# Inverting the unit triangles of a chunked delta rule column by column, with one product for the transposes of inverse and carried matrix

## The reference

```python
def step(state, inp):
    r_t, w_t, k_t, v_t, a_t, b_t = inp
    sa = jnp.einsum('bhvk,bhk->bhv', state, a_t)
    state = (state * w_t[:, :, None, :]
             + sa[..., None] * b_t[:, :, None, :]
             + v_t[..., None] * k_t[:, :, None, :])
    y_t = jnp.einsum('bhvk,bhk->bhv', state, r_t)
    return state, y_t
```

## Time and profile before

| | us |
|---|---|
| median of 3 runs | 2226.78 |
| lowest, highest | 2226.38, 2231.42 |
| profiled execution | 2220.09 |
| its span, first to last instruction | 2218.3 |

### The profile page before, as it was taken

How to read it: one execution, slowest core, us unless ns; L and a number is a source line. 1 busy time by engine, 2 the same in 40 slices (tenths; PEclk the granted TensorE clock), 3 DMA queues, 4 the chain that set the end, 5 groups by cost and what they waited for, 6 DMA issues and landing times.

```text
span 2218.3 us, 37433 instructions
## 1 busy us (share of the span) xinstructions
PE 2005.0 (90%) x15948; PEld 1570.5 (71%) x15948; DVE 792.4 (36%) x1248; ACT 812.1 (37%) x1061; POOL 777.7 (35%) x644
## 2 busy tenths in 40 slices
PE   5997976668999999989999899999999999979987
PEld 3666866643778888866667478888887886768767
DVE  5586443324332221014766632222102223324333
ACT  6766133332244343122247534343312423242232
POOL 3353322210334443433432034444444433234432
PEclk8998999986899999999999899999999999989988
DMA  5111000010223333222121022333223121131211
GB/s 154 57 50 63 2 5 5 4 48 23 59 75 94 99 90 109 95 80 67 65 69 39 0 76 76 97 92 102 97 91 106 60 77 57 39 100 58 77 38 58
DMA packets 190138, 147.16 MB, mean 66 GB/s; under 512 B 6826, under 2 KB 188289, under 8 KB 190004
## 3 DMA queue, kind: packets, MB, share of 16 engines
q1 hardware_dynamic: 190004, 145.18, 21.2%
HBM read 143.07 MB, written 2.10 MB: 65 GB/s over the span
## 4 chain that ended last, share of the span: by engine, by line
PE 79%; DVE 7%; ACT 5%; issue 5%; POOL 2%; DMA 1%; SPq 0%; DVEq 0%; ACTq 0%
PE psum L2479 21%; PE psum L2481 20%; PE psum L2480 20%; PE psum L2634 4%; POOL w_lo L1099 2%; ACT w_hi L1220 1%; DVE X_lo L1773 1%; PE psum L2555 1%; PE psum L2485 1%; PE psum L2859 1%; PE psum L2920 1%; PE psum L2933 1%; PE psum L2850 1%; PE psum L3030 1%; DVE col L2230 0%
## 5 line engine op out<-in xcount | busy, mean ns | idle before, releaser
L1099 POOL TENSOR_TENSOR w_lo<-weight_raw,w_hi 128x256 fp32r<-128x256 f32 (+5 forms) x588 | 706.1, 1233 | 1236.5 <-ACT w_hi L1220 1236.4
L2479 PE MATMUL psum<-X_hi,w_hi 128*128 128x512 f32 x1400 | 577.4, 412 | 26.3 <-DVE X_lo L1773 17.8
L2481 PE MATMUL psum<-X_hi,w_lo 128*128 128x512 f32 x1400 | 552.3, 395 | 0.0
L2480 PE MATMUL psum<-X_lo,w_hi 128*128 128x512 f32 x1400 | 551.9, 394 | 0.0
L1220 ACT ACTIVATE w_hi<-weight_raw 128x2048 fp32r<-128x2048 f32 (+2 forms) x134 | 249.5, 1862 | 362.9 <-PE psum L2481 338.3
L2479 PEld LDWEIGHTS psum<-X_hi,w_hi 128*128 128x128 f32 x1400 | 266.5, 190 | 126.8 <-issue 53.8
L2480 PEld LDWEIGHTS psum<-X_lo,w_hi 128*128 128x128 f32 x1400 | 266.8, 191 | 58.7 <-issue 7.5
L2481 PEld LDWEIGHTS psum<-X_hi,w_lo 128*128 128x128 f32 x1400 | 266.3, 190 | 58.1
L2479 PE MATMUL psum<-w_hi,X_hi 128*128 128x256 f32 x640 | 191.4, 299 | 13.0 <-DVE X_lo L1773 10.8
L2480 PE MATMUL psum<-w_lo,X_hi 128*128 128x256 f32 x640 | 185.1, 289 | 0.0
L2481 PE MATMUL psum<-w_hi,X_lo 128*128 128x256 f32 x640 | 184.9, 289 | 0.0
(11 more groups left out here) (465 smaller groups left out, 2566.3 us busy)
## 6 DMA issues: line engine op xcount, KB each, us to landing
weight_raw<-in_ffn_w_gu SPq DMA_DIRECT2D x88, 512.0 KB, 4.8
weight_raw<-in_l_w_in SPq DMA_DIRECT2D x45, 512.0 KB, 4.7
weight_raw<-in_ffn_w_down SPq DMA_DIRECT2D x40, 512.0 KB, 3.6
weight_raw<-in_kv_w SPq DMA_DIRECT2D x16, 512.0 KB, 4.5
weight_raw<-in_l_w_out SPq DMA_DIRECT2D x16, 512.0 KB, 4.5
weight_raw<-in_rw_w_k SPq DMA_DIRECT2D x8, 512.0 KB, 6.6
weight_raw<-in_rw_w_r SPq DMA_DIRECT2D x8, 512.0 KB, 4.0
weight_raw<-in_rw_w_v SPq DMA_DIRECT2D x8, 512.0 KB, 4.0
```

The lines of the kernel that those rows point to most:

```text
L1099: ins = pool.tensor_tensor(l, r, h.bitcast(F32), ALU.subtract)
L2479: pe.matmul(ps, wh, xh, start=start, stop=False, skip_group_check=True)
L2480: pe.matmul(ps, wh, xl, start=False, stop=False, skip_group_check=True)
L2481: return pe.matmul(ps, wl, xh, start=False, stop=stop, skip_group_check=True)
```

## The change

The triangle is inverted in another way. At level lv (0 to 5) blocks of 2^lv are joined to blocks of 2^(lv+1). A matrix N is carried along; the factor of a level is N under a mask that keeps the identity and takes away the pairs to be joined, `(j == i) - pair(n)`. Multiplying by this factor moves both the inverse and N one level on. So N of level lv (TensorE) times the factor gives the next factor under the next mask (VectorE), and one product, T, multiplies the factor with the transposes of inverse and N side by side: 128 columns instead of 64.

- AtX and its masks go. At is masked into the first stacked tile `TN0`, whose other part is the identity, written once by ScalarE; An is masked into the first factor, and VectorE adds the identity over 128x1024.
- N at levels 0 to 4, T at levels 0 to 5; T is 128 columns wide at levels 0 to 3, 64 at levels 4 and 5. Before, there were G and T at levels 1 to 5.
- The At copy on ScalarE and GpSimd's four level masks a tile go, with the semaphores for them. GpSimd's four identity additions stay, now before N0.
- The list of slots is rewritten; AV moves to the weight_raw region.

```diff
-LEVELS = (4, 8, 16, 32)
-CORE_MASKS = ("incl", "strict", "four_t", "four_n", "eye", "lv2", "lv3", "lv4", "lv5")
+LEVELS = (2, 4, 8, 16, 32)
+CORE_MASKS = ("incl", "strict", "minus", "pair0", "pair1", "pair2", "pair3", "pair4", "pair5")
...
-        "start": [("AtX", tt), ("An", tt), ("At", tt)],
+        "start": [("At", tt), ("An", tt)],
...
-    for name in ("start", "X0", "G1", "U0", "T1", "SY0", "G2", "YS0", "T2", "bt", "G3", "X1", "T3", "U1", "G4", "SY1",
-                 "T4", "YS1", "Ak", "G5", "Rb", "T5", "AV", "Rk", "kt"):
+    for name in ("start", "X0", "N0", "U0", "T0", "SY0", "N1", "YS0", "T1", "bt", "N2", "X1", "T2", "U1", "N3", "SY1",
+                 "T3", "YS1", "N4", "Ak", "T4", "Rb", "T5", "AV", "Rk", "kt"):
...
             for tt in range(TT):
-                wait_job(pool, ("AtX", tt))
+                wait_job(pool, ("At", tt))
                 for g in range(2):
                     for slot in range(2):
-                        part = TT2[1][:, g, slot, 1, :, :]
-                        pool.tensor_tensor(part, part, mask("eye", 4), ALU.add).then_inc(f_ready, 1)
-                pool.wait_ge(at_copied, tt + 1)
-                for lv in range(2, NLV + 1):
-                    if lv >= 3:
-                        wait_done(pool, ("G", tt, lv - 2, 1))
-                    elif tt:
-                        wait_done(pool, ("G", tt - 1, 4, 1))
-                    pool.tensor_tensor(whole(Lm[(lv + 1) % 2]), whole(At), mask(f"lv{lv}"),
-                                       ALU.mult).then_inc(level_ready, 1)
+                        part = TN0[:, g, slot, 1, :, :]
+                        pool.tensor_tensor(part, part, TN0[:, g, slot, 0, :, :], ALU.add).then_inc(unit_ready, 1)
...
+                        if what == "An":
+                            link(ins)
+                            dve.wait_ge(eye_ready, 1)
+                            every = Gs[0][:, :, :, :, :].rearrange("p g b k c -> p (g b) (k c)")
+                            ins = dve.tensor_tensor(every, every, TN0[:, :, :, 0, :, :].rearrange(
+                                "p g b k c -> p (g b) (k c)"), ALU.add)
...
+                        if what == "N":
+                            ins = product64(
+                                lambda q, r, k: psum[to(q, r)[0], b + to(q, r)[1], CH * k:CH * k + CH],
+                                lambda q, r, k: both[rows(q, r), g, level_slot(lv, q, r), 1, k, :],
+                                lambda q, r, k: factor[rows(q, r), g, level_slot(lv, q, r), k, :], ks=range(4))
+                        elif lv < NLV - 2:
+                            ins = product64(
+                                lambda q, r, k: psum[to(q, r)[0], b + to(q, r)[1], :].rearrange(
+                                    "p (t k c) -> p t k c", t=2, k=4)[:, :, k, :],
+                                lambda q, r, k: factor[rows(q, r), g, level_slot(lv, q, r), k, :],
+                                lambda q, r, k: both[rows(q, r), g, level_slot(lv, q, r), :, k, :], ks=range(4))
```

More of the change, by code:

```diff
@@ L100, in host_constants, with pair @@
     j, i = p[:, None] % 64, np.arange(64)[None, :]
[L101 to L104, removed]
+    def pair(n):
+        return 1.0 * ((j // (2 * n) == i // (2 * n)) & (j % (2 * n) >= n) & (i % (2 * n) < n))
+    masks = [j <= i, j < i, -1.0 * (j < i), pair(1)] + [(j == i) - pair(n) for n in LEVELS]
     lv = np.stack(masks, 1).astype(np.float32)
@@ L361, in core_slots @@
     mine = {
-        "start": [("AtX", tt), ("An", tt), ("At", tt)],
+        "start": [("At", tt), ("An", tt)],
         "Ak": [("Ak", tt)], "AV": [("AV", tt)], "Rb": [("Rb", tt)], "Rk": [("Rk", tt)], "kt": [("kt", tt)],
     }
-    for lv in range(1, NLV + 1):
-        for kind in "GT":
+    for lv in range(NLV):
+        for kind in "NT" if lv < NLV - 1 else "T":
             mine[f"{kind}{lv}"] = [(kind, tt, lv, 0), (kind, tt, lv, 1)]
@@ L403, in make_jobs @@
                 j.add(("bonus",), 5, "A")
-            elif what == "AtX":
-                j.add(("AtX", n), low, "D")
+            elif what == "At":
+                j.add(("At", n), low, "D")
             elif what == "An":
                 j.add(("An", n), high, "D")
[L408 to L411, removed]
+            elif what == "N":
+                j.add(("N", n, *lv), high if lv[1] else low, "D")
             elif what == "T":
@@ L910, in mask, with unit_mask, stacked @@
             return lvl[:, at_:at_ + 1, :].to_broadcast([P, n, CH])
-        def inverse(lv, g, kind):
-            return TT2[lv % 2][:, g, :, kind, :, :]
+        def unit_mask(name):
+            return lvl[:, None, CORE_MASKS.index(name), None, :].to_broadcast([P, 2, 4, CH])
+        def stacked(lv):
+            return TN0 if lv == 0 else TN[(lv + 1) % 2]
         def split_k(ap, g):
@@ L1472, in _ @@
             rn = xf[0:16, 1, :]
-            act.wait_ge(lvl_in, 16)
+            act.wait_ge(lo_ready, PL.first_slot["v"] + PL.count["v"])
+            for h in range(2):
+                at_ = CST["ident"] + CH * h
+                ins = act.activation(TN0[halves(h), :, :, 0, :, :].rearrange("p g b k c -> p (g b) k c"),
+                                     cst[halves(h), None, None, at_:at_ + CH].to_broadcast([CH, 4, 4, CH]), ACT.Copy)
+            ins.then_inc(eye_ready, 1)
             for tt in range(TT + 1):
@@ L2058, in _ @@
                                                  in1=kf[:, n, :], op0=ALU.mult, op1=ALU.mult).then_inc(bon_d, 1)
-                    elif what in ("AtX", "An"):
+                    elif what in ("At", "An"):
                         key = (what, n)
@@ L2062, in _ @@
                         b = job_banks(key)[0]
[L2063 removed]
                         for g in range(2):
[L2065 to L2075 removed]
+                            to = TN0[:, g, :, 1, :, :] if what == "At" else Gs[0][:, g, :, :, :]
@@ L2657, in _ @@
                                   start=n == 1, stop=n == KT).then_inc(bon_pe if n < KT else job_done, 1)
-                    elif what == "AtX":
-                        pairs("AtX", n, af, u0, lambda q, r: q ^ r)
                     elif what == "An":
```

113 lines of the change are left out of this document (43 added, 70 removed).

## The result

| us | before | after |
|---|---|---|
| median of 4 runs each | 2227.56 | 2209.70 |
| lowest, highest | 2226.38, 2231.42 | 2203.06, 2216.04 |
| profiled execution, its span | 2220.09, 2218.3 | 2216.04, 2213.2 |

The change makes the program faster by about 0.9%: the ratio to the kernel before is 0.9909, with a 95% interval of 0.9884 to 0.9934. By that ratio it is 20 us of 2227.6, with 15 to 26 in the interval; the medians of the four runs are 17.9 us apart. The forecast was 25.1. The profiled execution of the changed kernel is the slowest of its four, so its distance to the profile of before (4.1 us) understates the gain.

What follows compares the result with a forecast made beforehand. TensorE's instruction fetch, 3.75 us per block of 256, was taken as the bound. Tiles 1 to 3 save 21.6 us and tile 0 saves 3.5, together 25.1: 2226.8 - 25.1 = 2201.7 us, range 2192 to 2217.

Steps and rivals of the forecast that it cites:

- faster by over 0.3%: Whole program: a result below 2220.1 us, covering the forecast and nearly all of rival 1; chance 0.83.
- What bounds the stage: Tiles 1 to 3: the number of TensorE instructions, not columns; 14.1 blocks of 256 instructions make 53.0 us a tile.
- the price of a block: Tiles 1 to 3: 3.75 us per block of 256 instructions; two blocks fewer leave 12.1, 45.5 us a tile.
- Rival 2: Whole stage: blocks come late for a reason independent of their number, so nothing is gained; 2229 us, chance 0.06.
- The wide pass: New T at levels 0 to 3: 128-column passes go four abreast at 0.030 us each, leaving array time equal.
- Rival 3: New T: the wide product does not share the array, 0.112 us a pass; slower, 2265 us, chance 0.08.
- two-abreast form of rival 1: New T: wide passes go two abreast at 0.056 us, gaining 3.9 us a tile; rival 1, part gain, 2215 us, chance 0.14.
- Hand-overs in tiles 1 to 3: Between levels: six levels of 3.5 us are 21 us, under 45.5 of fetch; cost 0 while fetch is the bound.
- N0's chain: Tile start to N0: An and identity additions behind the At masks delay N0; 0.5 us a tile, 0 to 2.
- Tile 0: First token tile, nearly bound by the array with bonus sums between levels: gain 3.5 us, bounds 0 and 7.5.
- the 8.9 us for what stands behind N4: End of tile 0: 456 pairs, 7.8 us of array, up to 9.6 if one block of lead is left.
- the 5.3 us for the level from N0 to N1: Tile 0: a level takes 5.3 us, the old 6.6 put down to slow L2057; N0 at 268, N1 at 273.3.

Runs made afterwards that it cites:

- second profile: The changed kernel unedited, timed more often and profiled again; median 2204.7 us, ratio 0.9913 to the kernel before, profiled span 2204.9 us.
- split T: Each wide T product of the changed kernel issued as two of 64 columns, 256 more pairs a tile; median 2227.28 us, ratio 1.0020.
- kernel without sums: Seven of the eight bonus sums left out, in the changed kernel (2195.51 us) and in the kernel before (2219.41 us), one run each.
- merged Ak and Rk: Ak and Rk of the changed kernel made one 128-column product, 64 pairs fewer a tile; median 2202.85 us, ratio 0.9910.
- wide N: Each N product of the changed kernel computes its 64 columns twice, no instruction more; median 2208.0 us, ratio 0.9921.

## Why the prediction was right or wrong

The forecast of 2201.7 us was 8.0 us below the median of 2209.7, inside the range of 2192 to 2217, and faster by over 0.3% was the likely sign. By its own steps, from the two profiles of the changed kernel:

| us | before | forecast | first profile | second |
|---|---|---|---|---|
| tile 0 | 40.6 | 37.1 | 43.9 | 43.5 |
| tiles 1 to 3 | 159.6 | 138.0 | 146.5 | 138.7 |
| last chunks, to the next stage | 21.1 | 21.1 | 19.9 | 20.1 |

- **What bounds the stage, and the price of a block: right.** The packets went from 43 to 36, the second profile has 46.2 us a tile against 46.0, and the split T gives the old time back with the old count. The profile of before alone had shown it: resumptions in the middle of any product, at equal steps. "Mostly hidden" (the Trainium skill, Runtime: NRT & Kernel Launch, Instruction fetch mechanics) is refuted for this stage: 24.4 us of waits remain even after the change, and 22.6 us came back with the instructions. Rival 2 is out. The price of a block is that of an execution, though: 3.75 us between packets in the second profile, 3.99 in the first.
- **The wide pass: right.** 28 ns where 30 was taken; array time equal. Rival 3 is out, and so is the two-abreast form of rival 1.
- **Hand-overs in tiles 1 to 3: right that they stay covered**, but by less than the 21 us against 45.5 suggested. That sum looked at the levels alone, and a level without fillers, taken as 3.5 us, took 4.7 in the kernel without sums (N2 to N3; 3.7 for its neighbours less their filler). The merged Ak and Rk show hand-overs of AV, Rk and Gs half a block further on.
- **N0's chain: right in when N0 starts, wrong in what follows, in tile 0.** Without the additions N0 came 1.5 us earlier, and for tile 0 a start 6.2 us into the tile was used where 5.3 was measured. But GpSimd's additions were sized at 2.8 us and take 4.20, so the second half of N0 stands still for them, and the lower clock behind the longer wait was not in the sum at all. By the one run without them, the additions cost 5 us in tile 0, not 0 to 2. That the longer wait is what brought the clock down fits the runs, but none shows it by itself. What they cost in tiles 1 to 3 no run shows.
- **Tile 0: wrong, 6.4 to 6.8 us off.** Two steps failed: the 8.9 us for what stands behind N4, and the 5.3 us for the level from N0 to N1. The first profile against the reckoning: start to N0 5.3 for 6.2; N0 to N1 8.5 for 5.3; N1 to N4 15.8 for 16.7; N4 to the end 14.3 for 8.9. That is -0.9 + 3.2 - 0.9 + 5.4 = 6.8. The 6.6 us of the first level before had been put down to a slow L2057; in the timeline TensorE does not wait there, it runs at the lower clock (G of 1.76 us for 1.16, a sum of 1.89 for 1.03). Read so, it would have warned that a wait ahead of N0 costs more than itself.

The part behind N4 was reckoned as 456 pairs with a block of lead. There was none:

```profile
293.49 1.24 PE L2629 MATMUL psum<-Gs,TN 64*64 64x64 f32 x64
...
297.88 0.39 PE L2629 MATMUL psum<-TN,Gs 64*64 64x64 f32 x10 [1.39 <-issue]
...
301.70 0.45 PE L2629 MATMUL psum<-TN,Gs 64*64 64x64 f32 x14 [1.70 <-issue]
...
305.80 0.46 PE L2629 MATMUL psum<-rf,kf 64*64 64x64 f32 x15 [1.95 <-issue]
```

TensorE stops within the first 181 pairs, and then at steps of 3.8 and 4.1 us. 3.56 blocks at 3.75 are 13.4 us, near the measured 14.3. The row at 297.88 also tells why. The blocks ahead of it took some 5 us each, since sums and wide passes filled them, so a fetch that ran on during them would have had over 1 us in hand. Yet TensorE, which entered the block 128 pairs earlier, at about 294.3 (53 passes of 14.9 ns into N4), resumes 3.6 us after that: a whole fetch. The packets' records agree: between the levels of tile 0 they start 4.8 to 6.0 us apart in the two profiles, one for some 128 pairs, though one in 3.7 us is possible. Here are the instruction packets from 267 to 294 us, after and then before:

```profile
q8 instruction: 4, 0.07, 1.0%
```

```profile
q8 instruction: 7, 0.11, 1.9%
```

So, by this reading, the fetch of a block starts when the one before it is entered, and gains nothing while that one is slow. What a block loses to the array is not given back by the next: a stretch costs the sum over its blocks of the longer of 3.75 us and the block's own work, not the longer of the two sums.

The second question is why tile 0 did not gain on the kernel before at all. There start to G1, G1 to G5 and G5 to the end took 5.0, 25.7 and 9.9 us; the same parts to N0, to N4 and behind it now take 5.3, 24.3 and 14.3. Between the levels 1.4 us is won, and behind them stand 456 pairs for 328 (Ak and one T more). Before, a level in tile 0 had 64 + 128 = 192 pairs, 1.5 blocks or 5.6 us of fetch, beside 1.1 + 1.9 + 2 x 0.97 = 4.9 us of array. The two limits were nearly equal: TensorE shows no pause from 266.8 to 289.0 us, and its packets came 3.6 to 3.9 us apart. After, it has 128 pairs, 3.75 us, beside the same 4.9 us of array, which now sets the pace:

```profile
288.54 1.19 PE L2629 MATMUL psum<-Gs,TN 64*64 64x64 f32 x64
289.66 1.03 PE L2651 MATMUL psum<-xf,cst 128*16 128x512 f32 x2
290.62 1.98 PE L2629 MATMUL psum<-TN,Gs 64*64 64x128 f32 x64
292.53 1.03 PE L2651 MATMUL psum<-xf,cst 128*16 128x512 f32 x2
```

From N3 (288.54) to N4 (293.49) there is no gap. N1 to N3 take 10.87 us where the same two levels took 11.40, so 0.3 us a level is won where the count alone would give half a block, 1.9 us. The forecast had seen that tile 0 was "nearly bound by the array" and still credited most of a block there. The two runs without sums bear this out, but for 1.8 us over three levels and not for the whole 5.3 to 5.7. The rest of the loss is the start, 3.5 us between N0 and N1: 1.2 of GpSimd's additions and 2.3 of clock, of which the kernel before had 1.5. The split T shows the same from another side: with the old number of instructions the new order takes 4.8 us longer in tile 0 than the old one.

- **The other miss: a spread of executions.** Of the 8.0 us, tile 0 explains 6.4 to 6.8. The second profile's chip says the same: its medians are 18.2 us apart, 6.9 short of the forecast. The runs of the changed kernel lie between 2203.1 and 2216.0, those of before between 2226.4 and 2231.4. In the two profiles, the tiles 1 to 3 alone differ by 7.8 us, and there the packets took 1.16 and 1.045 us. Why packets are slow in one execution stays open.

Whether a version exists that beats the changed kernel is open too. The merged product had the lowest median beside it (2202.85 against 2204.7), within the error. By this reading the bonus sums would be free in tiles 1 to 3, where each block has array time left; in the present order their accumulation holds a PSUM bank that the state's chain needs there, and this was not tried.

## What to carry to other kernels

Where TensorE has no semaphore to wait for and resumes at equal steps in the middle of any product, count instructions, not columns: here a block of 256 cost about 3.7 us (3.3 by the split T) whatever it computed, as long as that took less, and one 128-column product in place of two of 64 halves the count. Sum over blocks the longer of fetch and work, and do not grant a lead. Work that hides behind such fetches is free only as long as the fetches are there: before taking instructions out, look for what was put beside them (here eight sums), and for how far the next limit is (here the next half block a tile brought nothing that could be measured). And look at what moves ahead of the first product of a chain: a wait there cost its own 1.5 us, and the lower clock behind it 2.3.

## What the runs showed of the hardware

- The fetch of TensorE's instructions does not get ahead by more than one block here. In stalled stretches a packet starts about 1.3 us after TensorE resumes, takes 0.9 to 1.5 us, and TensorE resumes some 1.4 us later; between the levels of tile 0, where nothing stalls, they are 4.8 to 6.0 us apart. About half of the packets last 0.9 to 1.0 us, the others anything up to 1.5, and the mix differs between executions (means of 1.00 to 1.16 us in tiles 1 to 3).
- Four 64x64 products with 128 columns share the array like those with 64: 28 and 14.9 ns a pass.
- GpSimd's four additions take 4.20 us in tile 0 of the changed kernel and 3.76 us in its later tiles. VectorE's addition runs beside them in both; what only tile 0 has is the first bonus product (L2053), and without it, in the run without sums, tile 0 has 3.76 us too.
- Behind 3.20 us without a product TensorE was granted 1.2 GHz for 6.8 us in both profiles of the changed kernel, and for 3.4 us in the runs with a wide N and without sums; behind 1.98 us, for 3.4 us in the kernel before, while the kernel before without sums had its 3.4 us only from 276.5 us on, 7 us after that wait; behind 1.73 us, in the kernel without additions, not at all.
